# Memory value pages of the samples: weighted and added on ScalarE and VectorE, or read one by one by TensorE

## The chip, the cores and the metric

The kernel runs on one core of one Trainium2 chip. The metric is the device time of the core in microseconds, the median of several runs. It is compared with runs of the kernel before on the same chip.

## The reference

One decoder layer for a prompt of 256 tokens and a group of 8 samples of one token each, which share all weights, in 32-bit floats. The stages are a half-step feed-forward, one projection into eight sections, three branches (block-sparse attention A, retention B, cross-attention to a memory C), gates, the output projection and a second half-step feed-forward. The part that is touched is branch C for the samples. Each sample attends to its own cached memory of 256 tokens with 4 heads of 256:

```python
def mem_attend(q, mk, mv):
    s = jnp.einsum('bqhd,bmhd->bhqm', q.astype(jnp.float32), mk.astype(jnp.float32)) * (M_DH ** -0.5)
    p = jax.nn.softmax(s, axis=-1)
    return jnp.einsum('bhqm,bmhd->bqhd', p, mv.astype(jnp.float32))
```

The last line is what is done in another way: for each of 8 samples and 4 heads, the sum over 256 memory tokens of a probability times a row of 256 values.

## The kernel before

The program is written out by hand, one instruction stream for each engine, with semaphores between them. The large products are split: each weight unit is loaded as 32-bit floats into `raw` (SyncE, L371), rounded by ScalarE into `splitH` (L503), its rest is made by VectorE into `splitL` (L509), and TensorE does three matmuls per weight tile (L554 to L556).

The middle of the kernel is one loop over T from 0 to 175, and each engine has its own copy of it. A unit T is one weight block of 8 row tiles, or of 4 in the projections of the gate stage, where T % 4 is 2 or 3 (T from 64 to 127). TensorE does unit T (`pe_mid_unit`) and then the side work of T (`pe_side`). ScalarE and VectorE split the weights of unit T + 2 first, evacuate, and then do the side work of T (`act_side`, `dve_side`). In the gate stage the split of a unit waits until TensorE has freed the half of the split buffer that it overwrites.

The samples' caches come in pages of 128 tokens by 1024 channels (512 KB), through a ring of five slots in SBUF (`ring`). GpSimd (POOL) issues the loads in one order, the list `PAGES`, which `uses()` (L1606) makes from the turns at which the pages are read. `sp_page` (L1636) waits until the slot's last page is used (`page_used`) and issues the load; the reader waits on `page_in` (`page_there`, L1675). Key pages are read by VectorE, half a page at a time, four or two multiply-and-reduce instructions (`dve_half_page`, L1681). From turn 82 on these are the key pages of samples 6 and 7 of branch A.

The memory value pages ("MV", two for each sample) stand between them. After turn 81 has made the probabilities (`dve_probs`, L1957), which are copied into `DM["one"]`, a tile of zeros with one column of eight filled for each sample, page and head, TensorE reads the pages behind units 83, 84, 86, 87, 89, 90, 92 and 93 (`MEM_AT`): `pe_mem_values` (L1976) does for each page and head a matmul with 8 columns of that tile as weights and 256 columns of the page as moving data. The four heads write four strips of 32 partitions of one PSUM bank, and all samples add up in it. A 32-bit matmul stands in the trace as two instructions. At the end ScalarE copies the bank (`act_row_copy`), TensorE turns it, VectorE takes it out (`dve_rows_out`), and `dve_decode_out` makes what unit 98 multiplies.

Of the kernel before, what the change touches and what calls it, by code (L numbers as in the profile page):

```python
# [7 lines left out]
ALU = mybir.AluOpType  # L8
ACT = mybir.ActivationFunctionType
# [31 lines left out]
RING, CHUNKS = 5, 5  # L41
# [42 lines left out]
def build(nc, d, o, sem, PS, block):  # L84
# [163 lines left out]
    def dec_tiles(kind, where, S, pages, heads):  # L248
# [66 lines left out]
    s_back = [sem(f"s_back{k}") for k in range(CHUNKS)]  # L315
    vb_in = [sem(f"vb_in{p}") for p in range(2)]
    s_scaled, s_new, s_read = map(sem, ("s_scaled", "s_new", "s_read"))
    r_all_done = sem("r_all_done")

    a_s, a_p, a_max, a_exp, a_norm, a_pt, a_ptc, a_o, a_hi, a_lo = map(sem, (  # L320
        "a_s", "a_p", "a_max", "a_exp", "a_norm", "a_pt", "a_ptc", "a_o", "a_hi", "a_lo"))
# [1 line left out]

    page_in = [sem(f"page_in{s}") for s in range(RING)]
    page_used = [sem(f"page_used{s}") for s in range(RING)]
    qb_in = [sem(f"qb_in{s}") for s in range(3)]
    gate_ps, sum_ps, d_sb, d_exp, d_max, d_maxall, d_logit, d_prob, m_done, a_done = map(sem, (
        "gate_ps", "sum_ps", "d_sb", "d_exp", "d_max", "d_maxall", "d_logit", "d_prob", "m_done", "a_done"))
    row_zero, row_sb, row_turned, row_out = map(sem, ("row_zero", "row_sb", "row_turned", "row_out"))


# [1183 lines left out]
    def act_row_copy(act, n):  # L1515

        if n == 0:
            act.wait_ge(st_sent[0], 32)
            act.wait_ge(st_sent[1], 32)
        if n >= 2:  # L1520
            act.wait_ge(row_turned, n - 1)
        nc.scalar.activation(row_tile(n)[:, n % 2, :, :], two(PS[:, 4, 0:2 * P]), ACT.Copy).then_inc(row_sb, 1)
# [53 lines left out]
    def dve_samp_out(dve, link):  # L1576

        dve.wait_ge(r_sqrt, R_HEADS + 1)
        link(nc.vector.reciprocal(RY, RT_))
        refine(link, RY, RV, RT_)  # L1580
        for et in range(2):
            last = nc.vector.tensor_tensor(orS2[:, et:BT:2, :], orS[:, et:BT:2, :],
                                           RY.rearrange("p (h b) -> p h b", h=R_HEADS), ALU.mult)
        link(last)
        link(nc.vector.tensor_tensor(orS2[:, :, :], orS2[:, :, :], grS[:, :, :], ALU.mult))
        dve.wait_ge(s_read, 2 * DEC)
        link(nc.vector.tensor_copy(orH[:, :, SEQ:N], orS2[:, :, :]))
        nc.vector.tensor_tensor(orL[:, :, SEQ:N], orS2[:, :, :], orH[:, :, SEQ:N].bitcast(F32),
                                ALU.subtract).then_inc(r_all_done, 1)


    KEYS = ([("A", b, g) for b in range(6) for g in range(NPAGES)] + [("M", b, g) for b in range(DEC) for g in range(2)]
# [13 lines left out]
    def uses():  # L1606

        at_slot, n = [], 0
        for T in sorted(KEY_AT):
            for _ in range(KEY_AT[T]):  # L1610
                n += 1
                if n % 2 == 0:
                    at_slot.append((T, 1, KEYS[n // 2 - 1]))
        for b, T in enumerate(MEM_AT):
            at_slot += [(T, 0, ("MV", b, g)) for g in range(2)]
        v = 0
        for T in sorted(VALUE_AT):
            for _ in range(VALUE_AT[T]):
                at_slot.append((T, 0, VALUES[v]))
                v += 1  # L1620
        return sorted(at_slot, key=lambda e: (e[0], e[1]))
# [31 lines left out]
    def page_read(eng, page):  # L1653

        n = PAGE_NO[page]
        eng.wait_ge(page_used[n % RING], n // RING + 1)
# [18 lines left out]
    def page_there(eng, page):  # L1675

        n = PAGE_NO[page]
        eng.wait_ge(page_in[n % RING], 16 * (n // RING + 1))
        return n % RING
# [277 lines left out]
    def dve_probs(dve, link, K):  # L1957

        t = K.t
        dve.wait_ge(sum_ps, K.q + 1)  # L1960
        tot = PS[:, sum_bank(K), 2 * P:2 * P + DEC * K.heads].rearrange("p (b h) -> p b h", b=DEC)
        if K is DKA:
            link(nc.vector.tensor_tensor(t["rd"][:, :, :], tot, t["eo"][:, :, :], ALU.add))
        else:
            link(nc.vector.tensor_copy(t["rd"][:, :, :], tot))
        link(nc.vector.reciprocal(t["x1"][:, :, :], t["rd"][:, :, :]))
        for g in range(K.pages):
            last = nc.vector.tensor_tensor(t["L"][:, :, g, :], t["L"][:, :, g, :], t["x1"][:, :, :], ALU.mult)
        if K is DKM:
            link(last)  # L1970
            w = K.pages * K.heads
            last = nc.vector.tensor_copy(t["one"][:, :].rearrange("p (b c) -> p b c", b=DEC)[:, :, 0:DEC * w:DEC],
                                         t["L"][:, :, :, :].rearrange("p b g h -> p b (g h)"))
        last.then_inc(d_prob, 1)

    def pe_mem_values(pe, b):  # L1976

        if b == 0:
            pe.wait_ge(d_prob, 1)
            pe.wait_ge(row_sb, MEM_ROWS)  # L1980
        for g in range(2):
            s = page_there(pe, ("MV", b, g))
            for h in range(M_HEADS):
                c0 = DEC * (M_HEADS * (2 * b + g) + h)
                last = nc.tensor.matmul(PS[32 * h:32 * h + DEC, 4, 0:M_DH], DM["one"][:, c0:c0 + DEC],
                                        ring[:, s, h * M_DH:(h + 1) * M_DH], start=b == 0 and g == 0,
                                        stop=b == DEC - 1 and g == 1)
            last.then_inc(page_used[s], 1)

    def pe_value_page(pe, k, g):  # L1990

# [6 lines left out]
                                    ring[:, s, 2 * j * P:2 * (j + 1) * P], start=g == 0, stop=g == NPAGES - 1)  # L1998
        last.then_inc(page_used[s], 1)

    def dve_decode_out(dve, link, K, done):
        t = K.t
        o_s = t["oS"][:, :, :]
        if K is DKA:

            link(nc.vector.tensor_tensor(t["eo"][:, :, :], t["eo"][:, :, :], t["x1"][:, :, :], ALU.mult))
            link(nc.vector.tensor_tensor(t["o2"][:, :, :], vaS[:, :, :], t["eo"][:, :, :].rearrange("p b h -> p h b"),
                                         ALU.mult))
            link(nc.vector.tensor_tensor(o_s, o_s, t["o2"][:, :, :], ALU.add))
        link(nc.vector.tensor_copy(K.oH[:, :, SEQ:N], o_s))  # L2010
        nc.vector.tensor_tensor(K.oL[:, :, SEQ:N], o_s, K.oH[:, :, SEQ:N].bitcast(F32),
                                ALU.subtract).then_inc(done, 1)


    def sigmoids(act, dst, t0, tile, section, pr):
# [74 lines left out]
    def pe_mid_unit(pe, T):  # L2090

        B, c, u, nk, gate = mid(T)
        if u % 2 == 0:
            pe_pair_free(pe, B, c, u)
        if T < 2:
            pe.wait_ge(h_ready, 8 + 4 * (T + 1))
        if 8 <= T < 10:
            pe.wait_ge(norm_lo, 2 * (T - 7))
        if T in (T_GATE + 2, T_GATE + 32 + 2, T_PROJ):
            pe.wait_ge((r_all_done, m_done, a_done)[(T - T_GATE) // 32], 1)  # L2100
        if T_OUT <= T < T_OUT + 2:
            pe.wait_ge(mg_lo, 4 * (T - T_OUT + 1))
        half = u % 2
        if T < 8:
            rhs = hH, hL
        elif T >= T_OUT:
            rhs = mgH, mgL
        elif T >= T_PROJ:
            rhs = BRANCHES[2][2]
        elif in_gates(T) and u >= 2:  # L2110
            rhs = BRANCHES[(T - T_GATE) // 32][2]
        else:
            rhs = gH, gL
        pe_unit(pe, B, c, u, rhs, range(half * nk, (half + 1) * nk), N, half == 0, half == 1, gate, T == T_OUT)
# [6 lines left out]
    def pe_side(pe, T, values):  # L2121
# [22 lines left out]
        if T == 81:  # L2144
            pe_prob_sums(pe, DKM)
        for b in range(DEC):
            if T == MEM_AT[b]:
                pe_mem_values(pe, b)
        if T == MEM_AT[DEC - 1] + 1:
            pe_row_turn(pe, MEM_ROWS)  # L2150
        if T == 99:
            pe_gate_sums(pe)
# [62 lines left out]
    def act_side(act, T, values):  # L2215
# [32 lines left out]
        act_heads(act, KM, T, MEM, 2, 6)  # L2248
        if T == 79:
            act_exps(act, DKM)  # L2250
        if T == MEM_AT[DEC - 1]:
            page_read(act, ("MV", DEC - 1, 1))
            act_row_copy(act, MEM_ROWS)
        act_heads(act, KA, T, MOBA, 3, 5)
        if T == 104:
            act_exps(act, DKA)
# [28 lines left out]
    def dve_side(dve, link, T, keys, values):  # L2285
# [49 lines left out]
            dve_sums(dve, DKM)  # L2335
        if T == 81:
            dve_probs(dve, link, DKM)
        if T == MEM_AT[DEC - 1] + 1:
            dve_rows_out(dve, MEM_ROWS, DM["oS"])
        if T == 95:  # L2340
            dve.wait_ge(row_out, PAST_ROWS)
            dve_decode_out(dve, link, DKM, m_done)
        if T == 99:
            dve_gates(dve, link)
            dve_blocks(dve, link, range(0, 2))
# [17 lines left out]
            dve_past_row_out(dve, DEC - 1, DA["oS"])  # L2363
        if T == 141:
            dve.wait_ge(row_out, PAST_ROWS + DEC)
            dve_decode_out(dve, link, DKA, a_done)
        if T_PROJ <= T < T_OUT and T % 2:
            last_proj_lo(dve, T)
        if T > T_OUT + 1 and T % 2:
# [5 lines left out]
        for _ in range(KEY_AT.get(T, 0)):  # L2375
            dve_half_page(dve, keys)
            keys += 1
        return keys, values

    def pool_pages(pool, T):  # L2380
# [21 lines left out]
    def pool_step(pool, T):  # L2402
# [34 lines left out]
            pool.wait_ge(turn_out, turns_to("va1"))  # L2437
            pool.dma_start(o["v_sample"], rows_va[0:DEC, :]).then_inc(v_sent, 16)
        if T == 76:
            pool.wait_ge(r_all_done, 1)  # L2440
            pool.wait_ge(v_sent, 16)
            pool.dma_start(mvTok[:, :, :], scratch["mv"].rearrange("(t p) c -> p t c", p=P)).then_inc(mv_in, 16)
        if T == 72:
# [7 lines left out]
            pool.wait_ge(v_sent, 32)  # L2451
            pool.dma_start(vaTok[:, :, :], o["v_prompt"].rearrange("(t p) c -> p t c", p=P)).then_inc(va_in, 16)
        if T == 101:
            pool.wait_ge(m_done, 1)
            pool.dma_start(biasD[:, :, :].rearrange("p g h -> p (g h)"), scratch["biasD"]).then_inc(biasD_in, 16)
            bias_rows(pool, 0)
            bias_rows(pool, 1)
# [226 lines left out]
```

## Time and profile before

| | us |
|---|---|
| median of 3 runs | 2694.39 |
| lowest and highest run | 2693.01 and 12234.96 |
| span of the profiled execution | 2688.8 |
| TensorE busy in it | 2662.4 |
| VectorE busy | 1541.8 |
| ScalarE busy | 1092.0 |
| GpSimd busy | 147.5 |

The span runs from the first to the last instruction on the core. The median of the timed runs is 5.6 us longer. The highest run stands far from the two others and is a disturbance. Matmuls are pipelined: one is some 0.28 us long in the trace, and the next starts about 0.12 us after it, so the busy time of one matmul is not what it adds. In the timeline, "idle before" in brackets is how long the engine had nothing to do ahead of that row, and what ended it.

### The profile page before, as it was taken

Reading aid. Unit: us, or ns where it says so; the run is one execution under the profiler, and the core shown is the slowest. Engines: PE = TensorE matmul, PEld = TensorE weight load, DVE = VectorE, ACT = ScalarE, POOL = GpSimd, SP = SyncE. Lnnn points to the kernel's source line nnn. Section 1 sums busy time; section 2 is a strip of 40 time slices with the busy share of each in tenths; the row PEclk is TensorE's granted clock in tenths of the full one; section 3 lists DMA queues with packets and bytes.
Section 4 is the critical chain, followed back from the end, with each engine's and each line's share of the span. In section 5 each row is a group of like instructions: output and inputs, shape, how many; then the busy total and the mean of one; then the engine's idle time right before and its main releaser. Section 6 shows DMA issues by size and latency. Waiting matters only on the chain.

```text
span 2688.8 us, 50855 instructions
## 1 busy us (share of the span) xinstructions
PE 2662.4 (99%) x21748; PEld 2590.7 (96%) x21748; DVE 1541.8 (57%) x2442; ACT 1092.0 (41%) x985; POOL 147.5 (5%) x266
## 2 busy tenths in 40 slices
PE   8999999999999999999999999999999999999998
PEld 7899999999999999999998988999999999999998
DVE  4545554555547778876675744365554545555455
ACT  6433333333335433455352444344433333333345
POOL 0000000000000011211211121100000000000000
PEclk9999999999999999999999999999999999999999
DMA  7665555555555799799979899766555555555553
GB/s 267 235 210 186 176 185 182 177 187 177 185 168 175 237 306 299 240 354 392 339 274 334 280 317 320 232 211 198 173 188 175 185 184 177 185 176 186 181 159 115
DMA packets 487449, 600.08 MB, mean 223 GB/s; under 512 B 12608, under 2 KB 447008, under 8 KB 485984
## 3 DMA queue, kind: packets, MB, share of 16 engines
q1 hardware_dynamic: 442512, 456.37, 52.9%
q0 software_dynamic: 35088, 129.74, 13.3%
q10 hardware_dynamic: 9680, 11.54, 1.2%
q8 instruction: 129, 2.11, 0.3%
q14 instruction: 40, 0.33, 0.0%
HBM read 575.16 MB, written 24.53 MB: 223 GB/s over the span
## 4 chain that ended last, share of the span: by engine, by line
PE 96%; DVE 1%; DMA 1%; ACT 1%; issue 1%; DVEq 0%; POOLq 0%; SPq 0%; ACTq 0%
PE PS L554 30%; PE PS L555 29%; PE PS L556 29%; PE PS L1997 1%; PE PS L590 1%; PE PS L592 1%; PE PS L591 1%; DVE splitL L509 1%; DMA raw<-w_gate 1%; ACT splitH L503 1%; PE PS L1760 0%; PE PS L1497 0%; PE PS L1728 0%; PE PS L1242 0%; PE PS L1356 0%
## 5 line engine op out<-in xcount | busy, mean ns | idle before, releaser
L509 DVE TENSOR_TENSOR splitL<-raw,splitH 128x2048 fp32r<-128x2048 f32 (+1 forms) x462 | 1007.5, 2181 | 841.8 <-ACT splitH L503 840.9
L503 ACT ACTIVATE splitH<-raw 128x2048 fp32r<-128x2048 f32 (+1 forms) x462 | 844.4, 1829 | 1493.4 <-PE PS L556 1443.4
L554 PE MATMUL PS<-gH,splitH 128*128 128x264 f32 x3072 | 880.9, 287 | 5.3 <-DVE splitL L509 5.3
L555 PE MATMUL PS<-gL,splitH 128*128 128x264 f32 x3072 | 871.2, 284 | 0.0
L556 PE MATMUL PS<-gH,splitL 128*128 128x264 f32 x3072 | 870.6, 283 | 0.0
L554 PEld LDWEIGHTS PS<-gH,splitH 128*128 128x128 f32 x3072 | 579.3, 189 | 25.0 <-issue 22.9
L555 PEld LDWEIGHTS PS<-gL,splitH 128*128 128x128 f32 x3072 | 579.7, 189 | 0.5 <-issue 0.2
L556 PEld LDWEIGHTS PS<-gH,splitL 128*128 128x128 f32 x3072 | 576.7, 188 | 0.0
L554 PE MATMUL PS<-hH,splitH 128*128 128x264 f32 x1536 | 436.1, 284 | 0.1
L555 PE MATMUL PS<-hL,splitH 128*128 128x264 f32 x1536 | 435.1, 283 | 0.0
L556 PE MATMUL PS<-hH,splitL 128*128 128x264 f32 x1536 | 434.9, 283 | 0.0
L554 PEld LDWEIGHTS PS<-hH,splitH 128*128 128x128 f32 x1536 | 289.2, 188 | 0.4 <-issue 0.3
L555 PEld LDWEIGHTS PS<-hL,splitH 128*128 128x128 f32 x1536 | 289.5, 188 | 0.1
L556 PEld LDWEIGHTS PS<-hH,splitL 128*128 128x128 f32 x1536 | 287.9, 187 | 0.0
L554 PE MATMUL PS<-hidH,splitH 128*128 128x264 f32 x704 | 200.8, 285 | 0.5 <-DVE splitL L509 0.2
L554 PE MATMUL PS<-hid2H,splitH 128*128 128x264 f32 x704 | 200.5, 285 | 0.3 <-DVE splitL L509 0.2
L555 PE MATMUL PS<-hidL,splitH 128*128 128x264 f32 x704 | 199.6, 283 | 0.0
L555 PE MATMUL PS<-hid2L,splitH 128*128 128x264 f32 x704 | 199.6, 283 | 0.0
L556 PE MATMUL PS<-hidH,splitL 128*128 128x264 f32 x704 | 199.3, 283 | 0.0
L556 PE MATMUL PS<-hid2H,splitL 128*128 128x264 f32 x704 | 199.3, 283 | 0.0
L1695 DVE CUSTOM_DVE_ANT_0 ring<-ring,qB 128x128 f32<-128x128 f32 (+1 forms) x560 | 132.0, 300 | 18.5 <-DMA ring<-cache_k 18.5
L554 PEld LDWEIGHTS PS<-hidH,splitH 128*128 128x128 f32 x704 | 132.6, 188 | 2.0 <-issue 1.1
(378 smaller groups left out, 2969.8 us busy)
## 6 DMA issues: line engine op xcount, KB each, us to landing
raw<-ffn_w SPq DMA_DIRECT2D x240, 1024.0 KB, 5.1
raw<-w_in SPq DMA_DIRECT2D x64, 1024.0 KB, 7.2
raw<-w_gate SPq DMA_DIRECT2D x48, 1024.0 KB, 8.0
ring<-cache_k POOLq DMA_DIRECT2D x64, 512.0 KB, 6.0
ring<-cache_v POOLq DMA_DIRECT2D x64, 512.0 KB, 5.8
raw<-ffn_w SPq DMA_DIRECT2D x32, 768.0 KB, 4.8
raw<-w_out SPq DMA_DIRECT2D x16, 1024.0 KB, 5.5
raw<-w_mem_kv SPq DMA_DIRECT2D x15, 1024.0 KB, 6.4
```

What stands on the lines that cost most here:

```text
L503: nc.scalar.activation(splitH[:, s, tiles, :], raw[:, u, 0:nk, :], ACT.Copy).then_inc(hi_ready, 1)
L509: nc.vector.tensor_tensor(splitL[:, s, tiles, :], raw[:, u, 0:nk, :], splitH[:, s, tiles, :].bitcast(F32), ALU.subtract).then_inc(split_re ...
L554: nc.tensor.matmul(out, w_hi, H[:, k, 0:n], start=first, stop=False)
L555: nc.tensor.matmul(out, w_hi, L[:, k, 0:n], start=False, stop=False)
L556: last = nc.tensor.matmul(out, w_lo, H[:, k, 0:n], start=False, stop=final)
L590: nc.tensor.matmul(out, t_hi, w_hi, start=u == 0 and j == 0, stop=False)
L591: nc.tensor.matmul(out, t_hi, w_lo, start=False, stop=False)
L592: last = nc.tensor.matmul(out, t_lo, w_hi, start=False, stop=u == 3 and j == 3)
L1695: last = nc.vector.tensor_tensor_reduce(k, k, query(Q_SLOT[j])[:, h * w:(h + 1) * w], 1.0, 0.0, ALU.mult, ALU.add, S[:, b, g, h:h + 1])
L1997: last = nc.tensor.matmul(PS[32 * j:32 * j + A_HEADS, 4, 0:2 * P], DA["L"][:, k, g, :], ring[:, s, 2 * j * P:2 * (j + 1) * P], start=g == ...
```

## The change

ScalarE multiplies page 1 of a sample by its probabilities, in place, one head at a time (`act_mem_product`). VectorE multiplies page 0 by its own and adds the product, in place (`dve_mem_sum`). TensorE reads only the sum, behind the next unit, with weights that are ones in one column (`DM["one"]` holds a single column of ones at 8, and the slice is shifted by the sample). VectorE frees page 1's slot, TensorE page 0's. In the list of pages the two value pages of a turn now come after the key pages of that turn, page 1 first. The row copy and row turn that follow the last sample, and `dve_decode_out`, move one unit later. Three semaphores for the end of the branches become one counter, `branch_done`.

```diff
         for b, T in enumerate(MEM_AT):
-            at_slot += [(T, 0, ("MV", b, g)) for g in range(2)]
+            at_slot += [(T, 1, ("MV", b, g)) for g in (1, 0)]
...
         if K is DKM:
             link(last)
-            w = K.pages * K.heads
-            last = nc.vector.tensor_copy(t["one"][:, :].rearrange("p (b c) -> p b c", b=DEC)[:, :, 0:DEC * w:DEC],
-                                         t["L"][:, :, :, :].rearrange("p b g h -> p b (g h)"))
+            last = nc.vector.memset(t["one"][:, DEC:DEC + 1], 1.0)
         last.then_inc(d_prob, 1)
 
+    def act_mem_product(act, b):
+        if b == 0:
+            act.wait_ge(d_prob, 1)
+        s = page_there(act, ("MV", b, 1))
+        for h in range(M_HEADS):
+            page = ring[:, s, h * M_DH:(h + 1) * M_DH]
+            last = nc.scalar.activation(page, page, ACT.Copy, scale=DM["L"][:, b, 1, h:h + 1])
+        last.then_inc(mv_prod, 1)
+
+    def dve_mem_sum(dve, b):
+        if b == 0:
+            dve.wait_ge(d_prob, 1)
+        s0 = page_there(dve, ("MV", b, 0))
+        s1 = PAGE_NO["MV", b, 1] % RING
+        dve.wait_ge(mv_prod, b + 1)
+        for h in range(M_HEADS):
+            page = ring[:, s0, h * M_DH:(h + 1) * M_DH]
+            last = nc.vector.scalar_tensor_tensor(page, page, DM["L"][:, b, 0, h:h + 1],
+                                                  ring[:, s1, h * M_DH:(h + 1) * M_DH], ALU.mult, ALU.add)
+        last.then_inc(page_used[s1], 1)
+
     def pe_mem_values(pe, b):
         if b == 0:
-            pe.wait_ge(d_prob, 1)
             pe.wait_ge(row_sb, MEM_ROWS)
-        for g in range(2):
-            s = page_there(pe, ("MV", b, g))
-            for h in range(M_HEADS):
-                c0 = DEC * (M_HEADS * (2 * b + g) + h)
-                last = nc.tensor.matmul(PS[32 * h:32 * h + DEC, 4, 0:M_DH], DM["one"][:, c0:c0 + DEC],
-                                        ring[:, s, h * M_DH:(h + 1) * M_DH], start=b == 0 and g == 0,
-                                        stop=b == DEC - 1 and g == 1)
-            last.then_inc(page_used[s], 1)
+        page_read(pe, ("MV", b, 1))
+        s = PAGE_NO["MV", b, 0] % RING
+        for h in range(M_HEADS):
+            last = nc.tensor.matmul(PS[32 * h:32 * h + DEC, 4, 0:M_DH], DM["one"][:, DEC - b:2 * DEC - b],
+                                    ring[:, s, h * M_DH:(h + 1) * M_DH], start=b == 0, stop=b == DEC - 1)
+        last.then_inc(page_used[s], 1)
...
         for b in range(DEC):
-            if T == MEM_AT[b]:
+            if T == MEM_AT[b] + 1:
                 pe_mem_values(pe, b)
-        if T == MEM_AT[DEC - 1] + 1:
+        if T == MEM_AT[DEC - 1] + 2:
             pe_row_turn(pe, MEM_ROWS)
...
-        if T == MEM_AT[DEC - 1]:
-            page_read(act, ("MV", DEC - 1, 1))
+        if T == MEM_AT[DEC - 1] + 1:
+            page_read(act, ("MV", DEC - 1, 0))
             act_row_copy(act, MEM_ROWS)
+        for b in range(DEC):
+            if T == MEM_AT[b]:
+                act_mem_product(act, b)
...
-        if T == 95:
+        if T == 96:
             dve.wait_ge(row_out, PAST_ROWS)
-            dve_decode_out(dve, link, DKM, m_done)
+            dve_decode_out(dve, link, DKM)
...
+        for b in range(DEC):
+            if T == MEM_AT[b]:
+                dve_mem_sum(dve, b)
         return keys, values
```

`dve_mem_sum` stands at the end of VectorE's side work, behind the half pages of the same turn.

## Rows read from the trace of the kernel before

**Rows 1.** The page: its span, TensorE's busy time, the chain by engine

```profile
span 2688.8 us, 50855 instructions
...
PE 2662.4 (99%) x21748; PEld 2590.7 (96%) x21748; DVE 1541.8 (57%) x2442; ACT 1092.0 (41%) x985; POOL 147.5 (5%) x266
...
PE 96%; DVE 1%; DMA 1%; ACT 1%; issue 1%; DVEq 0%; POOLq 0%; SPq 0%; ACTq 0%
```

**Rows 2.** Timeline of TensorE around units 84 and 87: start, duration, engine, line

```profile
1406.41 0.28 PE L556 MATMUL PS<-orH,splitL 128*128 128x264 f32 x1
1406.62 1.05 PE L1985 MATMUL PS<-ring,M_one 128*8 128x256 f32 x16
1407.60 0.39 PE L554 MATMUL PS<-gH,splitH 128*128 128x264 f32 x1
...
1413.60 1.05 PE L1985 MATMUL PS<-ring,M_one 128*8 128x256 f32 x16
...
1424.46 0.39 PE L554 MATMUL PS<-orH,splitH 128*128 128x264 f32 x1
...
1427.59 1.05 PE L1985 MATMUL PS<-ring,M_one 128*8 128x256 f32 x16
```

**Rows 3.** Timeline of ScalarE, GpSimd, VectorE and TensorE around unit 92

```profile
1440.47 0.85 ACT L2019 ACTIVATE EV<-PS,gT 128x264 f32<-128x264 f32 x2 [3.73 <-PE PS L556]
1441.22 1.91 ACT L503 ACTIVATE splitH<-raw 128x2048 fp32r<-128x2048 f32 x1
1442.23 0.53 POOL L1651 DMA_DIRECT2D ring<-cache_k  x1 [7.20 <-issue]
1448.44 0.29 DVE L1695 CUSTOM_DVE_ANT_0 ring<-ring,qB 128x128 f32<-128x128 f32 x1 [7.44 <-DMA ring<-cache_k]
1451.72 0.36 PE L554 MATMUL PS<-gH,splitH 128*128 128x264 f32 x1 [3.10 <-DVE splitL L509]
1453.50 0.42 PE L555 MATMUL PS<-gL,splitH 128*128 128x264 f32 x1
1459.25 1.05 PE L1985 MATMUL PS<-ring,M_one 128*8 128x256 f32 x16
```

**Rows 4.** Stretches: length, busy time of PE, PEld, DVE, ACT, POOL, clock, DMA

```profile
1450.00:1460.00 10.00, 8.28 (x64) 7.75 (x64) 6.10 (x19) 1.22 (x2) 0.53 (x1) 0.83 0.88 307
...
sum 80.00, PE 76.90 PEld 70.24 DVE 46.81 ACT 24.85 POOL 15.75; mean PE 9.61 PEld 8.78 DVE 5.85 ACT 3.11 POOL 1.97
```

**Rows 5.** Timeline of ScalarE and VectorE in the retention's state update

```profile
1162.70 1.33 ACT L1462 ACTIVATE chunk<-chunk 128x256 f32<-128x256 f32 x4
...
1165.64 1.67 DVE L1477 SCALAR_TENSOR_TENSOR chunk<-vB,krT,chunk 128x256 f32<-128x256 f32 x4
```

**Rows 6.** Timeline of VectorE and ScalarE in turn 83

```profile
1406.73 0.70 DVE L2045 TENSOR_TENSOR accT<-EV,PS 128x528 f32<-128x528 f32 x1 [0.76 <-PE PS L556]
1406.79 1.92 ACT L503 ACTIVATE splitH<-raw 128x2048 fp32r<-128x2048 f32 x1 [2.39 <-PE PS L556]
1408.74 2.29 DVE L509 TENSOR_TENSOR splitL<-raw,splitH 128x2048 fp32r<-128x2048 f32 x1 [1.30 <-ACT splitH L503]
1410.95 0.28 DVE L1695 CUSTOM_DVE_ANT_0 ring<-ring,qB 128x128 f32<-128x128 f32 x1
...
1411.79 0.09 DVE L1695 DVE_READ_ACCUMULATOR2_ANT S_A<- 128x1 f32 x1
```

**Rows 7.** Timeline: GpSimd's page loads and VectorE's first read of one

```profile
1412.17 0.53 POOL L1651 DMA_DIRECT2D ring<-cache_mem_v  x1 [2.32 <-DVE S_A L1695]
1415.46 0.53 POOL L1651 DMA_DIRECT2D ring<-cache_k  x1 [2.76 <-issue]
...
1462.28 0.53 POOL L1651 DMA_DIRECT2D ring<-cache_k  x1 [0.64 <-issue]
...
1468.43 0.29 DVE L1695 CUSTOM_DVE_ANT_0 ring<-ring,qB 128x128 f32<-128x128 f32 x1 [0.47 <-DMA ring<-cache_k]
```

**Rows 8.** The ring from 1390 to 1475 us: loads from issue to landing

```profile
DMA to landing us min/median/max: 3.6/6.1/9.6
```

More of the change, by code:

```diff
@@ L317, in build @@
     s_scaled, s_new, s_read = map(sem, ("s_scaled", "s_new", "s_read"))
-    r_all_done = sem("r_all_done")
     a_s, a_p, a_max, a_exp, a_norm, a_pt, a_ptc, a_o, a_hi, a_lo = map(sem, (
@@ L325, in build @@
     page_used = [sem(f"page_used{s}") for s in range(RING)]
+    mv_prod = sem("mv_prod")
     qb_in = [sem(f"qb_in{s}") for s in range(3)]
-    gate_ps, sum_ps, d_sb, d_exp, d_max, d_maxall, d_logit, d_prob, m_done, a_done = map(sem, (
-        "gate_ps", "sum_ps", "d_sb", "d_exp", "d_max", "d_maxall", "d_logit", "d_prob", "m_done", "a_done"))
+    gate_ps, sum_ps, d_sb, d_exp, d_max, d_maxall, d_logit, d_prob, branch_done = map(sem, (
+        "gate_ps", "sum_ps", "d_sb", "d_exp", "d_max", "d_maxall", "d_logit", "d_prob", "branch_done"))
     row_zero, row_sb, row_turned, row_out = map(sem, ("row_zero", "row_sb", "row_turned", "row_out"))
@@ L1588, in dve_samp_out @@
         nc.vector.tensor_tensor(orL[:, :, SEQ:N], orS2[:, :, :], orH[:, :, SEQ:N].bitcast(F32),
-                                ALU.subtract).then_inc(r_all_done, 1)
+                                ALU.subtract).then_inc(branch_done, 1)
     KEYS = ([("A", b, g) for b in range(6) for g in range(NPAGES)] + [("M", b, g) for b in range(DEC) for g in range(2)]
@@ L1999, in pe_value_page, with dve_decode_out @@
         last.then_inc(page_used[s], 1)
-    def dve_decode_out(dve, link, K, done):
+    def dve_decode_out(dve, link, K):
         t = K.t
@@ L2011, in dve_decode_out @@
         nc.vector.tensor_tensor(K.oL[:, :, SEQ:N], o_s, K.oH[:, :, SEQ:N].bitcast(F32),
-                                ALU.subtract).then_inc(done, 1)
+                                ALU.subtract).then_inc(branch_done, 1)
     def sigmoids(act, dst, t0, tile, section, pr):
@@ L2099, in pe_mid_unit @@
         if T in (T_GATE + 2, T_GATE + 32 + 2, T_PROJ):
-            pe.wait_ge((r_all_done, m_done, a_done)[(T - T_GATE) // 32], 1)
+            pe.wait_ge(branch_done, (T - T_GATE) // 32 + 1)
         if T_OUT <= T < T_OUT + 2:
@@ L2337, in dve_side @@
             dve_probs(dve, link, DKM)
-        if T == MEM_AT[DEC - 1] + 1:
+        if T == MEM_AT[DEC - 1] + 2:
             dve_rows_out(dve, MEM_ROWS, DM["oS"])
-        if T == 95:
+        if T == 96:
             dve.wait_ge(row_out, PAST_ROWS)
-            dve_decode_out(dve, link, DKM, m_done)
+            dve_decode_out(dve, link, DKM)
         if T == 99:
@@ L2365, in dve_side @@
             dve.wait_ge(row_out, PAST_ROWS + DEC)
-            dve_decode_out(dve, link, DKA, a_done)
+            dve_decode_out(dve, link, DKA)
         if T_PROJ <= T < T_OUT and T % 2:
@@ L2439, in pool_step @@
         if T == 76:
-            pool.wait_ge(r_all_done, 1)
+            pool.wait_ge(branch_done, 1)
             pool.wait_ge(v_sent, 16)
@@ L2453, in pool_step @@
         if T == 101:
-            pool.wait_ge(m_done, 1)
+            pool.wait_ge(branch_done, 2)
             pool.dma_start(biasD[:, :, :].rearrange("p g h -> p (g h)"), scratch["biasD"]).then_inc(biasD_in, 16)
```

## The prediction

> **What bounds the kernel now.** I read the page first. TensorE is busy in 2662.4 of 2688.8 us and carries 96% of the chain that ended last [rows 1]. So the change can move the time only where TensorE gets less to issue, or waits. Span and median stand 5.6 us apart (2688.8 against 2694.39, the median of three runs, whose lowest is 2693.01), and I keep these 5.6 us.
>
> Next the timeline of TensorE where the memory value pages are read. A "unit" T is one weight block, a "turn" T what ScalarE or VectorE do in their loop at T: they split the weights of unit T+2 first, so turn T runs while TensorE computes unit T+1. The reads stand behind units 83, 84, 86, 87, 89, 90, 92 and 93, x16 instructions each time, 0.98 us from the first to the next unit's start (1406.62 to 1407.60); a full unit takes 6.00 us (1407.60 to 1413.60), a half one about 3.0 to 3.1 (1424.46 to 1427.59) [rows 2]. Full are 84, 85, 88, 89, 92, 93, half are 86, 87, 90, 91, 94, 95.
>
> Last the waits of this stretch. There is one long one: VectorE waits 7.44 us for a key page whose slot a value page had held, its next split is late, TensorE stands idle for 3.10 us before unit 92, and from 1453.50 its matmuls take 0.42 us instead of 0.28; that stretch has granted clock 0.83 [rows 2 to 4]. Unit 92 runs from 1451.72 to 1459.25, 7.53 us, 1.53 more than a full unit. So the clock fell to its lower level, 1.2 GHz, and that wait cost 3.10 + 1.53 = 4.63 us.
>
> **TensorE's share.** 16 instructions become 8 per sample. At 0.98/16 = 0.061 us each that is 0.49 us per sample, 8 x 0.49 = 3.9 us [rows 2]. The eight waits for pages leave TensorE; it now waits for VectorE's sum at the end of unit T+1. Dropping the copy that spread the probabilities (one instruction on VectorE) and storing a one instead I cost at nothing: VectorE does it in turn 81, and waits there anyway.
>
> **The new work.** Its shapes are in the trace: four scaled ScalarE copies of 128x256 take 1.33 us together, four VectorE multiply-adds of 128x256 take 1.67 us [rows 5]. Eight times that (10.6 and 13.4 us) is no price by itself. The price is the time by which the sum misses the end of unit T+1, because behind it TensorE's queue stands.
>
> **The ring.** Key pages now stand ahead of the value pages of the same turn, and the second value page ahead of the first. Of the five slots, the one of page 1 is freed by VectorE's sum, the one of page 0 by TensorE one unit later: both are held longer than before. A slot freed lets POOL issue 0.29 us later for a value page (VectorE done 1411.88, issue 1412.17), 1.37 us later for a key page (TensorE's first eight end at 1414.09, issue 1415.46); a page lands after 3.6, 6.1, 9.6 us (least, median, most) [rows 2, 6 to 8]. I take 6.1.
>
> **The walk**, in the times of the trace before. A half page of keys is 0.93 us of VectorE (1410.95 to 1411.88), a full split 1.95 us on ScalarE up to VectorE's start and 2.21 on VectorE [rows 6], a half split about half of each; a pair of sigmoids 0.75 before the next ScalarE instruction (1440.47 to 1441.22) [rows 3].
>
> - *Sample 0.* Unit 84 starts at 1406.62 (no reads ahead of it) and ends at 1412.62. VectorE: split, two half pages (1412.81; the second no longer waits, its page is loaded earlier), sum to 1414.48. TensorE waits **1.9 us**. Unit 85 ends at 1420.97.
> - *Sample 1.* Its page 0 takes the slot of the key page done at 1411.88: issue 1412.17, landed 1418.27, sum 1419.94. **No wait**, 1.0 us to spare. Unit 86 ends at 1424.46, 87 at 1427.46.
> - *Sample 2.* Sigmoids after unit 85, split of 88, half page: 1426.81. The next key page has sample 1's slot: issue 1421.31, landed 1427.41; half page and sum end at 1430.0. TensorE waits **2.55 us** (1.95 if the page is early). Unit 88 ends at 1436.5.
> - *Sample 3.* Page 0 issued at 1427.1, landed 1433.2; the evacuation (0.70 us) [rows 6], split and half page last to 1433.85, the sum to 1435.5. **No wait**. Unit 89 ends at 1443.0.
> - *Sample 4.* ScalarE must first evacuate unit 89, then weight: 1445.1; sum 1446.75 against unit 90's end at 1446.0: **0.75 us**. The key page that was late before took its slot at 1435.5 and is there at 1443.0: the old wait before unit 92 is gone.
> - *Sample 5.* Split of 92, half page, sum: 1451.85 against 1450.25: **1.6 us**.
> - *Sample 6.* Sum at 1464.05, unit 93 ends at 1464.35: **no wait**.
> - *Sample 7.* VectorE's turn 93 has two half pages, and the second is of a key page that gets sample 6's slot: issue 1465.4. The same page took 6.15 us in the trace before (issue 1462.28, first read 1468.43) [rows 7]; the shortest load is 3.6. With 6.15: landed 1471.6, half page and sum to 1474.2; unit 94 ends at 1467.85. TensorE waits **6.35 us** (3.8 with 3.6).
>
> Waits: 1.9 + 2.55 + 0.75 + 1.6 + 6.35 = 13.15 us. Against that 3.9 saved and 4.63 of the old wait: +4.6 us. After the last wait, twice as long as the one of 3.10, I expect the clock to fall once as it did there: +1.53, so +6.1. The row turn and the final split move one unit on; VectorE has done the latter in about 3 us of the 6.0 of unit 97, so I cost them at nothing (uncovered they are under 1 us).
>
> **The clock.** The row shows one fall, after 3.10 us of idling; no row shows idling of 2 us between dense matmuls [rows 3]. The Trainium skill, "TensorE: Matmul & The Clock Gate", Part 1, says that the array's clock is released by activity and taken back when the engine idles, and it speaks against this change, which makes idle stretches. By the row alone I charge one fall, 1.53 us; by the page's rule the waits of 1.6 to 2.55 us might be charged too, up to 3 x 1.53 = 4.6 us more. I keep one fall, and both ends for the range.
>
> **The rivals.**
>
> *The gain stays (faster).* The sums are ready when TensorE comes, since VectorE is busy for 46.8 of 80 us of this stretch [rows 4] and the order of pages was the old trouble. Then 2694.4 - 3.9 - 4.6 = 2685.9 us. It needs VectorE to end 2 us earlier in turn 83 than the rows allow, where nothing but its own work stands in line, and sample 7's key page to come within some 1 us. Chance 0.2, mostly for shares of it.
>
> *Late pages (slower).* Place: the ring. Pages held longer make loads start later and crowd the queue with the weights. It decides where a page lands more than 7.1 us after its issue (samples 1 and 3, 1.0 us to spare each). With 9.6 us throughout: sample 1 waits 2.5, sample 3 some 2.5, sample 7 3.4 more, and two further falls 3.1: about +11.5 over my forecast, some 2712 us. Chance 0.2.
>
> *The clock falls at the short waits too.* 2700.5 + 4.6 = 2705 us; held inside my range, chance 0.1 of the 0.55 below. The page's rule named above is the one that would bring it.
>
> *The pages hide it anyway:* TensorE saves 3.9 and an equal wait takes its place, 2694. It lies between the first rival and the forecast; 0.05 goes to it and to what I don't see.
>
> **How the numbers follow.** Forecast: 2688.8 + 6.1 + 5.6 = 2700.5 us, chance 0.55, its own range 2695 to 2706 (with early pages and no fall +1.5, 2696; with the short falls 2705). Range for 8 in 10: 2688 to 2711, from shares of the first rival to nearly all of the second. Faster or slower by over 2% (about what a measurement of this kernel can tell from no change) would be 54 us, more than four times the sum of all waits above. No case reaches it: faster 0.01, within 2% 0.97, slower 0.02.
>
> **What would show it.** TensorE: x8 reads behind units 84, 85, 87, 88, 90, 91, 93, 94 at about 0.5 us. An idle of about 2 us behind units 84 and 87, ended by the multiply-adds; the longest, 4 to 6 us, behind 94, with VectorE waiting for a key page just before it, and a granted clock under 1.0 after it. The 3.10 us before unit 92 gone. If the idles are absent, my walk is wrong on VectorE; if they stand behind 85 and 88, on the pages' landing. If the time moves by over 15 us, something outside this stretch has changed.

## The result, and the profile after

The changed kernel takes 2702.35 us, the median of six runs (2700.77 to 2708.07), against 2694.1 us for the kernel before in runs beside them: a ratio (worked out from the single runs, not the quotient of the two medians) of 1.0033, with a 95% interval of 1.0023 to 1.0044. The forecast was 2700.5 us, 6.1 us more than before; measured are 8.25 us more. The page of the profile after, its span and busy times, to be held against [rows 1]:

```profile
span 2699.7 us, 50800 instructions
...
PE 2663.4 (99%) x21684; PEld 2593.3 (96%) x21684; DVE 1554.1 (58%) x2474; ACT 1104.2 (41%) x1017; POOL 147.5 (5%) x266
```

TensorE has 64 instructions fewer, yet the span is 10.9 us longer. VectorE is busy 12.3 us more and ScalarE 12.2; neither is near its limit. What the new order makes of it stands in TensorE's timeline after, at the reads of the sums (the last number in brackets is the idle before):

```profile
1416.78 1.04 PE L2004 MATMUL PS<-ring,M_one 128*8 128x256 f32 x8 [1.97 <-DVE ring L1993]
...
1418.14 0.42 PE L555 MATMUL PS<-gL,splitH 128*128 128x264 f32 x1
...
1424.89 0.62 PE L2004 MATMUL PS<-ring,M_one 128*8 128x256 f32 x8
1425.44 0.39 PE L554 MATMUL PS<-orH,splitH 128*128 128x264 f32 x1
...
1433.32 0.62 PE L2004 MATMUL PS<-ring,M_one 128*8 128x256 f32 x8 [1.79 <-DVE ring L1993]
1439.87 0.62 PE L2004 MATMUL PS<-ring,M_one 128*8 128x256 f32 x8
1450.79 0.62 PE L2004 MATMUL PS<-ring,M_one 128*8 128x256 f32 x8 [1.42 <-DVE ring L1993]
1455.58 0.62 PE L2004 MATMUL PS<-ring,M_one 128*8 128x256 f32 x8 [1.04 <-DVE ring L1993]
1467.95 0.62 PE L2004 MATMUL PS<-ring,M_one 128*8 128x256 f32 x8
1477.35 1.04 PE L2004 MATMUL PS<-ring,M_one 128*8 128x256 f32 x8 [5.68 <-DVE ring L1993]
```

L2004 is the read of a sum, L1993 the sum itself. Five of eight reads wait for it, 11.9 us in all. A read of eight instructions lasts 0.62 us, or 1.04 us where the clock fell: behind the first wait and behind the last. The stretches after (columns as in [rows 4]) show the same falls in the third number from the right, and none between:

```profile
1410.00:1420.00 10.00, 8.03 (x58) 7.00 (x58) 7.58 (x31) 6.23 (x11) 2.11 (x4) 0.84 0.58 190
...
1450.00:1460.00 10.00, 8.16 (x72) 7.09 (x73) 9.22 (x25) 4.28 (x6) 2.63 (x5) 1.00 0.86 307
...
1470.00:1480.00 10.00, 4.32 (x29) 3.26 (x29) 5.23 (x18) 2.66 (x4) 1.93 (x4) 0.74 0.62 216
1480.00:1490.00 10.00, 10.00 (x79) 10.00 (x78) 4.38 (x16) 2.78 (x2) 0.72 (x2) 0.92 0.84 295
```

The wait of 3.10 us ahead of unit 92 [rows 3] is gone. The longest wait is behind unit 94, and the timeline of GpSimd and VectorE after shows VectorE waiting for a key page just ahead of the last sum:

```profile
1469.12 0.53 POOL L1651 DMA_DIRECT2D ring<-cache_k  x1 [2.83 <-PE PS L2004]
...
1474.77 0.29 DVE L1695 CUSTOM_DVE_ANT_0 ring<-ring,qB 128x128 f32<-128x128 f32 x1 [4.89 <-DMA ring<-cache_k]
...
1475.63 1.67 DVE L1993 SCALAR_TENSOR_TENSOR ring<-ring,M_L 128x256 f32<-128x256 f32 x4
```

By the program this key page takes the slot that VectorE's sum of sample 6 frees, at 1467.90, and not one that TensorE frees: the profile's releaser, L2004, is TensorE's read of that sum, which starts 0.05 us later. The issue comes 1.22 us after the sum, where the forecast had 1.37.

To place the time, I cut each span in the same way. The first mark is TensorE's sum of the probabilities (L1954, one instruction pair, 1398.74 before and 1401.06 after); the second is its first read of `omH`, the tile that `dve_decode_out` completes and unit 98 multiplies (1484.9 and 1494.7); the third its last read of `omH` (1648.5 and 1658.2). Between the first two lies the changed stretch.

| us | ahead | changed stretch | next stretch | rest | span |
|---|---|---|---|---|---|
| before | 1398.7 | 86.2 | 163.6 | 1040.3 | 2688.8 |
| after | 1401.1 | 93.6 | 163.5 | 1041.5 | 2699.7 |

The changed stretch holds 7.4 of the 10.9 us between the two spans. The 2.3 us ahead of it were mostly lost at one place, which executions of one program pass differently: TensorE idled 2.05 us for a weight split at 1340.86 after, with a granted clock of 0.83 in 1340 to 1350, and 1.38 us at 1347.58 before, with 1.00. In a second profile of the kernel before, the first mark stands at 1400.28, 1.5 us later than in the first. I don't charge these 2.3 us to the change.

### The profile page after: what moved, and what is told of

The parts are those of the page before. It is cut to its first block, busy times and chain, and to the rows that moved or that the text cites. A ratio compares the mean times of both kernels' runs of the same rounds, so it can differ in the third digit from the quotient of the medians.

```text
span 2699.7 us, 50800 instructions
## 1 busy us (share of the span) xinstructions
PE 2663.4 (99%) x21684; PEld 2593.3 (96%) x21684; DVE 1554.1 (58%) x2474; ACT 1104.2 (41%) x1017; POOL 147.5 (5%) x266
## 4 chain that ended last, share of the span: by engine, by line
PE 94%; DVE 2%; DMA 1%; ACT 1%; issue 1%; SPq 0%; DVEq 0%; POOLq 0%; ACTq 0%
PE PS L554 29%; PE PS L555 29%; PE PS L556 29%; PE PS L2015 1%; DVE splitL L509 1%; PE PS L590 1%; PE PS L592 1%; PE PS L591 1%; ACT splitH L503 1%; DMA raw<-w_gate 1%; DMA raw<-w_mem_kv 0%; PE PS L1760 0%; PE PS L1728 0%; PE PS L1497 0%; DVE ring L1993 0%
```

## The experiments

Theory: the time is lost because sums come late, the last one behind a key page, and by the clock behind the waits. Rivals: the ring's order is what costs, or TensorE's saved instructions matter more than the waits. Times are medians; ratios, worked out from the single runs, are to the kernel before beside them. The runs below were made on three chips, on which the kernel before took 2694.12, 2693.88 and 2694.03 us, so I compare rows across them; "stretch" and "next" are as in the table above, and the waits are TensorE's in the changed stretch, without those for splits. Stretch, next and waits come from one profiled execution of each kernel.

| run | us | ratio, 95% interval | waits for sums or pages | stretch | next |
|---|---|---|---|---|---|
| e1_sum_first | 2699.73 | 1.0020 [1.0011, 1.0029] | 10.9 | 93.7 | 163.5 |
| e2_turn93 | 2695.96 | 1.0005 [0.9996, 1.0014] | 8.4 | 88.2 | 163.5 |
| e3_order_only | 2703.43 | 1.0033 [1.0021, 1.0045] | 9.6 | 95.0 | 163.5 |
| e4_half_sum | 2697.42 | 1.0011 [1.0002, 1.0020] | 9.3 | 89.6 | 163.5 |
| e5_twice | 2703.2 | 1.0031 [1.0020, 1.0042] | 10.1 | 94.8 | 163.9 |
| e6_between | 2696.0 | 1.0006 [0.9997, 1.0015] | 8.2 | 88.2 | 163.5 |
| e7_between_act | 2691.56 | 0.9990 [0.9981, 0.9999] | 4.9 | 84.1 | 164.3 |
| before_again | 2692.96 | 1.0 [0.9991, 1.0009] | 0 | 84.4 | 163.7 |
| e8_before_later_half | 2693.87 | 0.9993 [0.9984, 1.0002] | 0 | 81.5 | 168.9 |
| e9_before_late_v | 2689.34 | 0.9984 [0.9975, 0.9993] | 0 | 81.3 | 163.7 |
| e10_act_late_v | 2697.47 | 1.0013 [1.0004, 1.0022] | 4.4 | 82.9 | 170.0 |

**The sum ahead of the key half pages.** In the changed kernel's VectorE side work, the loop with `dve_mem_sum` moves up.

```diff
+        for b in range(DEC):
+            if T == MEM_AT[b]:
+                dve_mem_sum(dve, b)
         for _ in range(KEY_AT.get(T, 0)):
             dve_half_page(dve, keys)
             keys += 1
-        for b in range(DEC):
-            if T == MEM_AT[b]:
-                dve_mem_sum(dve, b)
```

> The changed kernel, with VectorE's sum put ahead of the key half pages of its turn. Theory (TensorE waits because VectorE's own queue puts one or two half pages, and in turn 93 a key page that is still loading, ahead of the sum): the waits behind units 84 and 87 (1.97 and 1.79 us) lose up to two half pages, 1.86 us, and go to about 0; behind 91 (1.04) to about 0.1; behind 90 (1.42) about 1.0 stays, since there ScalarE evacuates unit 89 before it weights; behind 94 (5.68) about 0.6 is left. Sum 11.9 to about 2 us, and the two falls of the clock (1.5 us each) go: 2702.4 - 10 - 3 = 2689 us, below the kernel before. Rival (the value pages themselves come too late, since the ring holds pages longer): the waits stay at 8 to 12 us, now ended by loads, 2698 to 2703 us.

The first sum was ready almost in time (0.27 us of wait instead of 1.97), but the waits add up to 10.9 us again. Half pages that come later free their slots later: the second value page load behind the first mark was issued 15.0 us after it (1415.26 - 1400.24), against 13.4 in the changed kernel. VectorE's waits ahead of the sums in this run (us in all, how many, the longest):

```profile
DVE ring L1993 <- DMA ring<-cache_mem_v: 9.4, 4, 3.7
DVE ring L1993 <- ACT ring L1981: 7.3, 2, 6.8
```

Four sums now wait 9.4 us for a value page. The pages take the place of the queue on VectorE, as the rival said: the longest TensorE waits are 2.86, 2.62 and 2.22 us, behind units 88, 91 and 94, and the clock falls behind each of these three.

**One key half page moved from turn 93 to turn 94** in the changed kernel, the one the last sum stood behind.

```diff
-              90: 1, 91: 1, 92: 2, 93: 2, 94: 1, 95: 1, 96: 2, 97: 2, 98: 1}
+              90: 1, 91: 1, 92: 2, 93: 1, 94: 2, 95: 1, 96: 2, 97: 2, 98: 1}
```

> The changed kernel, with one half page of keys moved from turn 93 to turn 94, so that nothing in turn 93 waits for the key page that takes the slot freed by the sum before. Theory: the wait behind unit 94 falls from 5.68 to about 1 us and the fall of the clock after it goes: 2702.4 - 4.7 - 1.5 = 2696 us, the other four waits as they were. Rival (the long wait is the page's lateness, wherever it is read): TensorE waits as long behind unit 95 or 96, and the time stays at 2702.

Met: 6.4 us less than the changed kernel. TensorE's reads in this run, the first, third and last:

```profile
1417.56 0.62 PE L2004 MATMUL PS<-ring,M_one 128*8 128x256 f32 x8 [1.98 <-DVE ring L1993]
...
1434.04 1.04 PE L2004 MATMUL PS<-ring,M_one 128*8 128x256 f32 x8 [3.30 <-DVE ring L1993]
...
1474.56 0.62 PE L2004 MATMUL PS<-ring,M_one 128*8 128x256 f32 x8 [0.64 <-DVE ring L1993]
```

The last wait went from 5.68 to 0.64 us, with its fall of the clock. So the key page ahead of the last sum is shown as the cause of that wait. The third read's wait grew from 1.79 to 3.30 here, with a fall of its own: VectorE waits 1.42 us for a key page just ahead of that sum. The first wait, 1.98 us, was not followed by a fall; 1.97 us after was. These two nearly cancel, so that the time met the forecast to 0.04 us is in part luck; the last row above is the evidence.

**The new order of pages alone**, in the kernel before: TensorE still reads all pages itself, page 0 first.

```diff
-            at_slot += [(T, 0, ("MV", b, g)) for g in range(2)]
+            at_slot += [(T, 1, ("MV", b, g)) for g in range(2)]
```

> The kernel before, with the new order of the ring alone: key pages ahead of the value pages of the same turn; TensorE still reads both value pages behind unit T. Theory (the wait of 3.10 us before unit 92 came from the order, a key page that needed a slot held by a value page of the turn before): it goes, with the fall of the clock behind it: 2694.1 - 4.6 = 2689.5 us. Rival (it went because the sums slow TensorE down and give the load time): the wait stays, 2694 us, or stands elsewhere on a value page.

The old wait went, as expected, but two longer ones came, for value pages that now load behind the key pages:

```profile
1418.18 0.62 PE L1985 MATMUL PS<-ring,M_one 128*8 128x256 f32 x8 [3.94 <-DMA ring<-cache_mem_v]
...
1438.44 1.04 PE L1985 MATMUL PS<-ring,M_one 128*8 128x256 f32 x8 [4.53 <-DMA ring<-cache_mem_v]
```

The clock fell behind both: behind the first it came about 1 us after the read's start, so the read itself still lasts 0.62 us, but the granted clock of the 4 us from 1418.18 is 0.60. This order costs the kernel before as much as the whole change does (95.0 us of stretch against 93.6). The order that cures the wait for a key page makes one for the value pages. Reading one unit later, as the change does, should give the pages that time back, which is then spent on the sums; this last is my reading, no run tests it alone.

**Half the product and half the sum**: heads 0 and 1 alone, in both functions, so the output of the two other heads is left out.

```diff
-        for h in range(M_HEADS):
+        for h in range(M_HEADS // 2):
```

> The changed kernel with only two of the four heads weighted and added (two heads' output is left out): the sum on VectorE is 0.83 us shorter, the product on ScalarE 0.8 us. Theory (TensorE waits for the engines' own work): every wait is shorter by at least 0.83 us: 1.97 to 1.1, 1.79 to 0.9, 1.42 and 1.04 to 0.2 or less, 5.68 to 4.9; sum 11.9 to about 7.2, and the fall behind unit 84 goes: 2702.4 - 4.7 - 1.5 = 2696 us. Rival (pages): no change of the waits, 2702.

Some 0.85 us less on each engine for each sample shortens the waits behind 84, 87, 90 and 91 from 1.97, 1.79, 1.42 and 1.04 to 1.18, 1.70, 0 and 0.95 us, but the last stays at 5.45 of 5.68. So the theory holds in part: the waits add up to 9.3 us, not to 7.2. Behind 84 the wait falls by what the sum is shorter, and the fall of the clock there goes; behind 87, where VectorE now waits 0.60 us for a key page, and behind 91 it hardly moves. The length of the new work is one part, and late pages another that doesn't depend on it.

**TensorE reads each sum twice**, the second time with weights of zero.

```diff
-                                    ring[:, s, h * M_DH:(h + 1) * M_DH], start=b == 0, stop=b == DEC - 1)
+                                    ring[:, s, h * M_DH:(h + 1) * M_DH], start=b == 0, stop=False)
+        for h in range(M_HEADS):
+            last = nc.tensor.matmul(PS[32 * h:32 * h + DEC, 4, 0:M_DH], DM["one"][:, 2 * DEC:3 * DEC],
+                                    ring[:, s, h * M_DH:(h + 1) * M_DH], start=False, stop=b == DEC - 1)
```

> The changed kernel, in which TensorE does the eight instructions of each sample a second time with weights of zero, so 16 instead of 8 per sample as in the kernel before, and all waits are left in. Theory (a read of a page costs TensorE 0.49 us per sample, and the units behind it move by as much): 8 x 0.49 = 3.9 us more than the changed kernel, 2702.4 + 3.9 = 2706 us. Rival (the saving is lost in the waits, TensorE only waits less): no change, 2702.

The 64 instructions that the change had saved are back, and the median rises by 0.85 us, the stretch by 1.2, which is nearer to the rival's 2702 than to 2706. The waits fell from 11.9 to 10.1 us. While TensorE has to wait for a sum anyway, most of what it does ahead of that only shortens the wait.

**The sum between the two half pages of its turn**, in the changed kernel:

```diff
-        for _ in range(KEY_AT.get(T, 0)):
+        for i in range(KEY_AT.get(T, 0)):
             dve_half_page(dve, keys)
             keys += 1
-        for b in range(DEC):
-            if T == MEM_AT[b]:
-                dve_mem_sum(dve, b)
+            if i == 0 and T in MEM_AT:
+                dve_mem_sum(dve, MEM_AT.index(T))
```

> The changed kernel, with VectorE's sum behind the first half page of its turn and ahead of the second, so that the half page that frees a slot stays on time and the half of the next key page comes after the sum. It changes turns 83, 86, 89, 92 and 93. Theory (VectorE's order, with slots freed on time): behind 84 from 1.97 to 1.0, behind 87 from 1.79 (3.30 in the kernel with the turn 93 moved) to 0.9, behind 90 as it was (1.4, ScalarE's evacuation), behind 91 up to 1.9, since a half page is now done there, behind 94 to 0.6; sum about 6 us against 8.4 of the kernel with turn 93 moved, and no fall: 2692 us. Rival (any shift of half pages makes the value pages late, as with the sum put ahead of both): sum 9 to 11 us, 2698.

It takes 6.4 us less than the changed kernel, and 4 us more than expected. The last wait is 0.67 us; one of 2.32 us came behind unit 88, where the sum waits for a page, with a fall of the clock behind it, and VectorE waits 7.3 us for ScalarE's products, 6.56 of it for that of sample 4.

**That and the product ahead of ScalarE's evacuation:**

```diff
-        for b in range(DEC):
-            if T == MEM_AT[b]:
-                act_mem_product(act, b)
...
+            if T in MEM_AT:
+                act_mem_product(act, MEM_AT.index(T))
```

> As the one before, and ScalarE weights a page ahead of its evacuation in turns 89 and 93, not after it. Theory: the wait behind 90 goes (the sum is then ready at about unit 89's end plus 1 us), behind 91 it falls to 0.5 or less; waits of 2 to 3 us in all: 2694.1 - 3.9 - 4.6 + 2.5 = 2688 us, below both kernels. Rival (pages): waits of 6 us or more stay, 2692 to 2698.

The waits are 4.9 us, none above 1.33 and none with a fall of the clock behind it, and the stretch, 84.1 us, is the first of the changed kernel's that is no longer than that of before. The expected 2688 was not reached, but the median lies below both kernels. What remains lost in the changed kernel is order, then: the same instructions, in other places, take 10.8 us less, and 0.1% less than the kernel before (the interval's upper end, 0.9999, lies close to no gain).

**The kernel before once more**, for a second profile.

> The kernel before once more, for a second profile. If the wait of 3.10 us ahead of unit 92 belongs to the order of the pages, it is there again with 2 to 4 us and the fall of the clock behind it; if it was chance of one execution, it is missing. The time is that of the kernel before, about 2694 us.

The timeline of TensorE around unit 92 in it, and the clock of the stretches there:

```profile
1453.07 0.36 PE L554 MATMUL PS<-gH,splitH 128*128 128x264 f32 x1 [2.91 <-DVE splitL L509]
1459.04 1.05 PE L1985 MATMUL PS<-ring,M_one 128*8 128x256 f32 x16
```

```profile
1450.00:1455.00 5.00, 2.09 (x18) 1.96 (x17) 5.00 (x19) 1.91 (x1) 0.53 (x1) 1.00 0.82 294
1455.00:1460.00 5.00, 5.00 (x50) 4.23 (x49) 2.44 (x9) 0.79 (x1) 0.00 (x0) 1.00 1.00 346
```

The wait is there again, 2.91 us, but unit 92 lasts 5.97 us (1453.07 to 1459.04) instead of 7.53, at full clock. So the wait belongs to this program, not to one execution, and the fall behind it does not always come; that it comes from the order of the pages and of VectorE's reads is shown by the run with the new order and by the next one, in both of which it is gone. The stretch is 84.4 us here, 1.8 less than in the first profile.

**The old wait taken away alone.** In the kernel before, one key half page goes from turn 89 to turn 90, so that the late page is not wanted ahead of unit 92's split.

```diff
-              76: 1, 77: 1, 78: 1, 79: 2, 80: 2, 81: 1, 82: 1, 83: 2, 84: 1, 85: 1, 86: 2, 87: 1, 88: 1, 89: 2,
-              90: 1, 91: 1, 92: 2, 93: 2, 94: 1, 95: 1, 96: 2, 97: 2, 98: 1}
+              76: 1, 77: 1, 78: 1, 79: 2, 80: 2, 81: 1, 82: 1, 83: 2, 84: 1, 85: 1, 86: 2, 87: 1, 88: 1, 89: 1,
+              90: 2, 91: 1, 92: 2, 93: 2, 94: 1, 95: 1, 96: 2, 97: 2, 98: 1}
```

> The kernel before, with one half page of keys moved from turn 89 to turn 90, behind the split of unit 92. Theory (its one long wait is VectorE standing in front of that split for a key page, and is worth 3.10 + 1.53 us): the wait before unit 92 and the fall of the clock after it go: 2694.1 - 4.6 = 2689.5 us. Rival (the page is late for the chain wherever it is read): TensorE waits before unit 93 or 94 for as long, 2694.

The wait went (stretch 81.5 us, 4.7 less than in the first profile of before, 2.9 less than in the second), and the time did not (2693.87 us; the single runs spread from 2687.33 to 2698.71, wider than in any other row of the table): the next stretch is 5.3 us longer. There, in the profiled execution, ScalarE now waits for weights, and TensorE for the split behind them:

```profile
1491.53 1.92 ACT L503 ACTIVATE splitH<-raw 128x2048 fp32r<-128x2048 f32 x1 [7.50 <-DMA raw<-w_gate]
...
1495.83 0.39 PE L554 MATMUL PS<-gH,splitH 128*128 128x264 f32 x1 [1.43 <-DVE splitL L509]
...
1510.35 0.56 PE L554 MATMUL PS<-gH,splitH 128*128 128x264 f32 x1 [2.57 <-DVE splitL L509]
```

The value pages of branch A (`cache_v`) had begun to load at 1467.51 us; from 1480 to 1490 the DMA engines were busy throughout (share 1.03, 395 GB/s), and the weights had to share them. That alone proves nothing: they are as busy there in the first profile of before (1.04, 380 GB/s), where TensorE waits for no split over 0.5 us. The next run is the test.

**The same, and no value page of branch A loaded ahead of turn 104.** The line in the list of load turns:

```diff
-        LOAD_AT[n] = max(LOAD_AT[n], LOAD_AT[n - 1])
+        LOAD_AT[n] = max(LOAD_AT[n], LOAD_AT[n - 1], 104 if PAGES[n][0] == "V" else 0)
```

> The kernel before with a key half page of turn 89 moved to turn 90 (as in the run e8), and no value page of branch A loaded ahead of turn 104. Theory: what e8 saved in the stretch (4.9 us) was given back behind it because page loads of the next branch crowded the weight loads at 1475 to 1510 us; with those loads later TensorE's waits of 1.43 and 2.57 us for splits there vanish, and the time is about 2689.5 us, 4 to 5 us under the kernel before. Rival: the weights are late there for another reason; the waits stay and the time is that of e8, about 2694 us.

Met: 2689.34 us, the next stretch back at 163.7. The pages now start at 1477.29, and where a weight block was taken up by ScalarE at 1491.53 in e8, it is taken up at 1485.96 with no wait for its load:

```profile
1485.96 1.91 ACT L503 ACTIVATE splitH<-raw 128x2048 fp32r<-128x2048 f32 x1 [3.22 <-PE PS L556]
```

This is the fastest version of all, 0.16% under the kernel before. The DMA engines are again busy from 1480 to 1490 (1.02, 399 GB/s), so the two runs do not differ in how much is moved there; TensorE's longest wait for a split in the next stretch is 0.62 us. This version holds nothing of the change. The line without the moved half page was not run, so how much of the 0.16% each brings is open.

**The same line on top of the product and the sum in better places.**

> The run e7 (the changed kernel, sum between the two half pages of its turn and the product ahead of ScalarE's evacuation) with no value page of branch A loaded ahead of turn 104. Theory: as e7 in the stretch (about 5 us of waits left for the sums) and up to 1 us less behind it, about 2690.5 us. Rival, loads behind the stretch don't matter for this order of pages: 2691.6 us, as e7. If holding the value pages back makes the next branch late, over 2694 us.

Here the line hurts: 2697.47 us, with the next stretch at 170.0. The pages held back left GpSimd in one burst, four of them between 1484.09 and 1487.57, some 7 us later than in e9, where four left between 1477.29 and 1481.56, and TensorE stood still for a split whose weights came late:

```profile
1511.83 0.56 PE L554 MATMUL PS<-gH,splitH 128*128 128x264 f32 x1 [4.18 <-DVE splitL L509]
```

So "later pages are better" is not what e9 shows. My reading is that it counts whether they collide with a weight block that is wanted soon. It is not shown: the stretch is also shorter here than in e7 (82.9 against 84.1 us), and in e8 a shorter stretch alone went with a longer next one. Which date suits e7 was not tried, so whether the change gains anything when all loads are well placed stays open.

## Why the prediction was right, and where it was off

**The walk** is the step that carried the forecast, and it held read by read, each wait to within 0.8 us:

| behind unit | 84 | 85 | 87 | 88 | 90 | 91 | 93 | 94 | sum |
|---|---|---|---|---|---|---|---|---|---|
| forecast, us | 1.9 | 0 | 2.55 | 0 | 0.75 | 1.6 | 0 | 6.35 | 13.15 |
| measured, us | 1.97 | 0 | 1.79 | 0 | 1.42 | 1.04 | 0 | 5.68 | 11.9 |

It named the three reads without a wait, the longest wait and the key page behind it. That page took 5.65 us from issue to its first read (1469.12 to 1474.77), against the 6.15 that I took from [rows 7]. Behind 87 the key page came early, the case for which the walk had 1.95 us.

**The price of the product** was mis-sized: 1.33 us for four instructions, from [rows 5]; measured are 1.70. In that row the factor was a constant of the instruction, here it is read from a tile, one for each partition. ScalarE and VectorE after, in turn 89:

```profile
1446.52 0.85 ACT L2037 ACTIVATE EV<-PS,gT 128x264 f32<-128x264 f32 x2 [4.47 <-PE PS L556]
1447.26 1.70 ACT L1981 ACTIVATE ring<-ring,M_L 128x256 f32<-128x256 f32 x4
...
1449.07 1.67 DVE L1993 SCALAR_TENSOR_TENSOR ring<-ring,M_L 128x256 f32<-128x256 f32 x4 [1.76 <-ACT ring L1981]
```

The excess is 0.37 us for four, 0.09 for one. The Trainium skill, "ScalarE: Activation LUTs", section "What ACT_TABLE_LOAD costs", gives about 93 ns for each operand of an activation that is a pointer to a column; this trace agrees, and by it the term would have been right (1.33 + 4 x 0.093 = 1.70 us). The sum of sample 4 waits for just this product, behind the evacuation, and the wait behind unit 90 is 1.42 us instead of 0.75. The multiply-adds took 1.67 us as forecast.

**TensorE's share:** a read takes 0.55 us up to the next unit's start (1424.89 to 1425.44), where I had 0.49, so eight samples save 8 x (0.98 - 0.55) = 3.4 us and not 3.9. The run with doubled reads shows that most of this saving could not show in the time anyway.

**The old wait** of 4.63 us was a price of one execution. The second profile of before has 2.91 us and no fall. Measured against it, the change lengthens the stretch by 9.2 us instead of 7.4.

**The clock:** I charged one fall and two came, the one I named behind unit 94 and one behind the first wait. The price was right: from the first read to the second are 8.11 us after and 6.55 in the run with the moved half page (1417.56 to 1424.11), where it did not fall, so 1.56 us against the 1.53 forecast. The rival with falls at all short waits is wrong for this execution: none behind 1.79, 1.42 and 1.04.

With these sizes: 11.9 + 2 x 1.56 - 3.4 - 4.63 = 7.0 us, against 7.4 in the stretch. The remaining 0.4 I have not placed. That the forecast's +6.1 lies so near is luck in part: its waits are 1.25 us too long, and the fall that it left out is 1.56.

**Around the span:** I added 5.6 us to a profiled execution. Between a span and the time of its own run lie 1.6 us (2699.7 and 2701.34 after); the rest, some 4 us, is that the profiled execution of before, by its span, was quicker than the median. Such differences, about 2 us ahead of the stretch alone, are as large as the terms of my sum; part of the agreement to within 2 us is luck.

**The rivals.** The gain did not stay: the order of pages alone, which I thought was "the old trouble", costs 9 us in the kernel before. Late value pages didn't decide here (no wait behind 85 and 88), but they did as soon as the order on VectorE changed, in the runs with the sum first and between.

## What to carry to other kernels

When work moves from the bottleneck to engines with time to spare, walk the turn in which each result is wanted: it is less the work's length that counts than what stands ahead of it on its engine, here a half page whose load came late. A ring of pages is a schedule; one place in its order moves waits from one reader to another. And a wait removed ahead of a stretch that is bound by loads is given back there, unless the loads move too.

## What the hardware showed that I had not expected

An idle of nearly the same length lowers TensorE's clock in one execution and not in another: 1.97 us was followed by reads at 1.2 GHz after (1.04 us), 1.98 us was not in e2 (0.62 us); 3.10 us was in one profile of before, 2.91 us was not in the other. The Trainium skill, "TensorE: Matmul & The Clock Gate", Part 1, says of the start of a kernel that the same kernel can show a different number of slow matmuls from run to run; these rows show the like behind an idle in the middle of one.

But it is no even chance. Between 1335 and 1520 us of the thirteen traces TensorE stands idle 24 times for 1.83 us or more. Behind 22 of these the granted clock of the next 4 us is 0.50 to 0.68; the two others are the 1.98 and the 2.91 us just named, with 1.00. Behind the 35 idles from 0.90 to 1.79 us there it stays at 1.00 each time. So in a sum like the one above each wait near 2 us or longer should carry a fall, at 1.5 us each, and the exception is the chance.

An activation with its factor in a tile costs 0.09 us more than one with a constant, 23% at 128x256 (0.498 us for one in the profile after against 0.406 in the retention's update before).
